# One tile of a gather stage handled in two halves of 64 tokens, with its small pieces of work moved between the dots

## The reference

```
q      = (xt @ wq).reshape(T, 8, 2, 128)
scores = einsum('thcd,hcnd->thcn', q, keys)
s_top, i_top = top_k(scores, 16)
cand     = s_top[:, :, 0, :, None] + s_top[:, :, 1, None, :]
best, pos = top_k(cand.reshape(T, 8, 256), 16)       # idx = the 16 experts of each head
gate = softmax(best)
hid  = gelu(einsum('td,thkd->thk', xb, U[idx]))      # U: 16384 x 2048
out  = einsum('thk,thkd->td', gate * hid, Vt[idx])   # Vt: 16384 x 2048
```

## Time and profile before

| | us |
|---|---|
| median of 3 runs | 2131.49 |
| lowest and highest | 2127.75, 2134.61 |
| profiled execution, its own time | 2132.88 |
| its span | 2131.1 |
| PE busy | 1480.5 (69%) |
| DVE busy | 1619.7 (76%) |
| ACT busy | 872.1 (41%) |
| POOL busy | 969.6 (46%) |

### The profile page before, as it was taken

One profiled execution on the slowest core, in us unless ns is written; L12 is line 12 of the kernel. 1 busy time (PEld: TensorE's weight loads), 2 busy tenths in 40 slices (PEclk: granted clock), 3 DMA queues, 4 the chain that ended last, 5 costly groups with the idle time before them and its releaser, 6 DMA issues.

```text
span 2131.1 us, 26457 instructions
## 1 busy us (share of the span) xinstructions
PE 1480.5 (69%) x9809; PEld 1371.6 (64%) x9809; DVE 1619.7 (76%) x2122; ACT 872.1 (41%) x1116; POOL 969.6 (46%) x699
## 2 busy tenths in 40 slices
PE   6999999999999999910000002211358999999997
PEld 6987998898999889910000002211347999999996
DVE  5465764545644556789999999877888999899997
ACT  4354432344333444211211226577655444444443
POOL 1002220000000000178888878888866776667763
PEclk9999999999999999965555555555589999999998
DMA  5555344434455554699999999999917999999996
GB/s 202 177 178 194 139 139 138 153 135 158 158 178 178 198 178 167 250 361 422 421 422 408 416 369 411 412 421 417 419 52 263 357 358 358 350 358 359 359 358 229
DMA packets 151818, 597.85 MB, mean 281 GB/s; under 512 B 14720, under 2 KB 14736, under 8 KB 118288
## 3 DMA queue, kind: packets, MB, share of 16 engines
q0 software_dynamic: 58048, 356.02, 42.0%
q1 hardware_dynamic: 93648, 240.22, 32.0%
HBM read 594.09 MB, written 2.10 MB: 280 GB/s over the span
## 4 chain that ended last, share of the span: by engine, by line
PE 47%; issue 20%; POOL 13%; DVE 13%; DMA 5%; ACT 1%; POOLq 0%; DVEq 0%; SPq 0%; ACTq 0%; PEldq 0%
PE acc L1608 8%; PE acc L1611 8%; PE acc L1610 8%; POOL slots L495 6%; POOL starts L534 5%; DVE slots L1397 5%; PE acc L1625 3%; PE acc L1627 3%; PE acc L1626 3%; DMA starts<-in_v_gather,expert 2%; DMA slots<-in_peer_u,expert 2%; PE acc L1922 2%; PE scr L1924 2%; PE acc L1924 2%; PE scr L1922 2%
## 5 line engine op out<-in xcount | busy, mean ns | idle before, releaser
L881 DVE TENSOR_TENSOR w_lo<-raw,w_hi 128x2048 fp32r<-128x2048 f32 x136 | 314.7, 2315 | 302.8 <-ACT w_hi L550 301.8
L1397 DVE SCALAR_TENSOR_TENSOR slots<-slots,acc 128x2048 f32<-128x2048 f32 x188 | 424.7, 2285 | 46.6 <-DMA slots<-in_peer_u,expert 44.4
L550 ACT ACTIVATE w_hi<-raw 128x2048 fp32r<-128x2048 f32 x136 | 260.1, 1913 | 428.7 <-PE acc L1611 286.5
L534 POOL DMA_INDIRECT starts<-in_v_gather,expert x256 | 343.8, 1343 | 158.9 <-issue 81.3
L495 POOL DMA_INDIRECT slots<-in_peer_u,expert x256 | 250.9, 980 | 260.6 <-DVE expert L1369 148.4
L1608 PE MATMUL acc<-hT_hi,w_hi 128*128 128x256 f32 x1024 | 294.6, 288 | 3.0 <-PE acc L1611 1.7
L503 POOL TENSOR_TENSOR slots<-slots,N 128x2048 f32<-128x2048 f32 x62 | 280.7, 4528 | 31.5 <-DMA slots<-in_peer_u,expert 31.2
L843 ACT ACTIVATE v_hi<-v_raw 128x1408 fp32r<-128x1408 f32 x128 | 177.0, 1384 | 284.3 <-PE scr L1924 213.1
L1610 PE MATMUL acc<-hT_lo,w_hi 128*128 128x256 f32 x1024 | 292.1, 285 | 0.0
L1611 PE MATMUL acc<-hT_hi,w_lo 128*128 128x256 f32 x1024 | 291.9, 285 | 0.0
L746 ACT ACTIVATE slots<-slots 128x2048 f32<-128x2048 f32 x62 | 118.4, 1910 | 366.7 <-POOL slots L503 366.7
(11 more groups left out here) (284 smaller groups left out, 3341.9 us busy)
## 6 DMA issues: line engine op xcount, KB each, us to landing
raw<-in_w_in SPq DMA_DIRECT2D x88, 1024.0 KB
v_raw<-in_v_dense SPq DMA_DIRECT2D x128, 704.0 KB
raw<-in_w_o SPq DMA_DIRECT2D x16, 1024.0 KB
raw<-in_peer_wq SPq DMA_DIRECT2D x16, 1024.0 KB
raw<-in_w_a_up SPq DMA_DIRECT2D x8, 1024.0 KB
raw<-in_w_b_up SPq DMA_DIRECT2D x8, 1024.0 KB
slots<-in_peer_u,expert POOLq DMA_INDIRECT x256, 9.2
starts<-in_v_gather,expert POOLq DMA_INDIRECT x256
```

What stands on the lines that cost most here:

```text
L534: pool.indirect_dma_start(starts[s % CRING][:, :], None, v_gather[:, :], bass.IndirectOffsetOnAxis(ap=expert[:, s // NSEL, s % NSEL:s % NS ...
L550: a.activation(w_hi[:, m % 2, :, :], raw[:, m % 2, :, :], ACT.Copy).then_inc(hi_ready, 1)
L881: v.tensor_tensor(w_lo[:, m % 2, :, :], raw[:, m % 2, :, :], w_hi[:, m % 2, :, :].bitcast(fp32), ALU.subtract).then_inc(lo_ready, 1)
L1397: v.scalar_tensor_tensor(out=slots[j][:, :], in0=slots[j][:, :], scalar=1.0, in1=row, op0=ALU.mult, op1=ALU.mult, accum_out=hid_sum[:, t, ...
```

## The change

Tile 1 is gathered in two halves. In the first half (q = 128 to 191, phase 1) the 128 partitions hold tokens 0 to 63 of the tile twice, and a gather brings two choices of each of 64 tokens; in the second (q = 192 to 255, phase 2) the same for tokens 64 to 127. The number of gathers and their size stay.

- SP makes the doubled indices (`expert_twice`) and copies: tokens 0 to 63 of N1 twice into a new buffer `rows_twice`, then tokens 64 to 127 of N1 over tokens 0 to 63. In phase 1 ACT also copies `rows_twice` to N1's tile 0, for POOL's products.
- `rows_to_psum` runs three times, for phases 0, 1 and 2.
- The dots of a half lie on two sets of partitions; PE brings them together (`fold_hid`), once for the first half and once for both, and DVE reads the result from PSUM.
- `weights` is cut into `shift_gate`, `scale_gate`, `curve_in` and `curve_out`, which stand in groups 29, 30, 32 and 33 for tile 0, in groups 46, 47, 48 and 49 for tile 1's softmax and its first half; the last curve stands after the last dot.
- 48 of the 64 batches of scatters stand in the gather stage: one a group from 35, two a group from 43 to 62. 16 stay behind the last dot. POOL makes the first one-hots of most of them as soon as rows 249 and 250 are used; two are made ahead by ACT in groups 62 and 63.
- The ring of row buffers is ten to q = 123, eight to q = 203, and from q = 204 seven in the order of LATE_ROWS, three of them new. Row 127 goes to DVE, not to POOL.
- `weight_of1` is laid out by halves, [2, 128, 64]; `e_hi` and `e_lo` read it so.

```diff
+FIRST_TEN, LAST_TEN = 10, 124
+LAST_EIGHT = 204
+LATE_ROWS = (6, 7, 8, 11, 12, 9, 10)
+PHASES = (0, NSEL, NSEL + NSEL // 2, GATHERS)
+IN_GATHERS = SCATTERS - BATCHES // 2
-SPREAD_FROM, SPREAD_TWICE = 35, 57
+SPREAD_FROM, SPREAD_TWICE, SPREAD_END = 35, 43, 63
-AHEAD_FROM = 47
+AHEAD_FROM, AHEAD = 62, 2
+SHIFTED_AT = (29, 46)
...
     if q < LAST_TEN:
-        return (q - FOUR) % len(ROW_AT)
-    return 2 + (q - LAST_TEN) % SLOTS
+        return (q - FOUR) % FIRST_TEN
+    if q < LAST_EIGHT:
+        return 2 + (q - LAST_TEN) % SLOTS
+    return LATE_ROWS[(q - LAST_EIGHT) % len(LATE_ROWS)]
...
+    def until(g):
+        late = SPREAD_END - SPREAD_TWICE
+        return (max(0, min(g, SPREAD_TWICE) - SPREAD_FROM)
+                + max(0, min(g, SPREAD_END) - SPREAD_TWICE) * (IN_GATHERS - SPREAD_TWICE + SPREAD_FROM) // late)
+
+    return range(until(g), until(g + 1))
+
+def weighted_first(n):
+    return n < IN_GATHERS and (n < ACT_WEIGHTS or n % 3 == 0)
...
+            def double_experts(pair):
+                sp.wait_ge(expert_ready, 4 + pair + 1)
...
+                for u in range(2):
+                    for r in range(2):
+                        sp.dma_start(expert_twice[r * HALF:(r + 1) * HALF, u, cs]...
+            double_experts(0)
+            sp.wait_ge(h2_ready, NT)
+            for r in range(2):
+                sp.dma_start(rows_twice[r * HALF:(r + 1) * HALF, :], N1[0:HALF, 1, :]).then_inc(rows_in, 16)
+            sp.wait_ge(rows_in, 32)
+            sp.dma_start(N1[0:HALF, 1, :], N1[HALF:P, 1, :]).then_inc(rows_in, 16)
...
+            for j in (11, 12):
+                pool.wait_ge(row_used[j], uses_before(GATHERS, j))
+            for n in range(AHEAD, BATCHES // 2):
                 if maker(n) == "pool":
...
+            def curve_in(w):
+                z, h = dots_of(w), hid[:, 0, :]
+                if w:
+                    dve.wait_ge(hid_landed, w)
+                    link(v.tensor_copy(z, hid_ps))
...
+                link(v.tensor_tensor(h, z, z, ALU.mult))
+                link(v.tensor_scalar(h, h, TANH_A * TANH_B, TANH_A, ALU.mult, ALU.add))
+                v.tensor_tensor(h, h, z, ALU.mult).then_inc(tanh_in, 1)
...
             for i in range(GROUPS):
                 for q in range(FOUR * i, FOUR * i + FOUR):
                     if q >= FOUR and not on_pool(q):
                         dot(q)
+                    if q % FOUR == 0 and q in (PHASES[1] + FOUR, PHASES[2] + FOUR):
+                        curve_out(phase_of(q) - 1)
...
-                if i == GROUPS // 2 + 1:
-                    weights(0)
-                    dve.sem_inc(h_used, 1)
-                if i == GROUPS // 2 + 2:
-                    copy_gate(0)
+                for t in range(NT):
+                    if i == SHIFTED_AT[t]:
+                        shift_gate(t)
+                    if i == SHIFTED_AT[t] + 1:
+                        scale_gate(t)
+                    if i == PHASES[t + 1] // FOUR + 1:
+                        copy_gate(t)
                 if i == IJ_GROUP:
                     copy_ij(1)
-                for n in spread(i):
-                    hot_second(0, n)
-            weights(1)
+                for m in spread(i):
+                    hot_second(m)
+                for w in range(NT):
+                    if i == PHASES[w + 1] // FOUR:
+                        curve_in(w)
+            curve_in(2)
+            curve_out(2)
...
+            def fold_hid(w):
+                pe.wait_ge(ij_ready, NT)
+                pe.wait_ge(gateT_ready, w)
...
+                for r in range(2):
+                    rows = slice(r * HALF, (r + 1) * HALF)
+                    to = hid_ps.rearrange("p (h r k) -> p h r k", h=H, r=2)[:, :, r, :]
+                    for u in range(w):
+                        last = t_.matmul(to, (ident if u == r else turned)[rows, :], ...
+                    if r == 0:
+                        last.then_inc(half_folded, 1)
+                        pe.wait_ge(half_folded, w)
+                last.then_inc(hid_landed, 1)
...
-            for n in range(BATCHES):
-                if n == spread(IJ_GROUP)[0]:
+            for m in range(IN_GATHERS):
+                if m == spread(IJ_GROUP)[0]:
                     turn_ij(1)
-                scatter(0, n)
-            turn_gate(1)
-            for n in range(BATCHES):
-                scatter(1, n)
+                if m == spread(PHASES[2] // FOUR + 1)[0]:
+                    fold_hid(1)
+                    turn_gate(1)
+                scatter(m)
+            fold_hid(2)
+            turn_gate(2)
+            for m in range(IN_GATHERS, SCATTERS):
+                scatter(m)
```

More of the change, by code:

```diff
@@ L260, in build @@
         hot_a, hot_b = carve("hot_a", 2, SC, P), carve("hot_b", 2, SC, P)
[L261 removed]
+        hot_a1 = [at(f"hot_a1_{n}", kib, [SC, P]) for n, kib in enumerate(PLACE_AT)]
         spot = [0]
@@ L485, in gather @@
                 t, k, j = q // NSEL, q % NSEL, buffer_of(q)
-                if k % (2 * TOPK) == 0:
+                index = expert_twice[:, k // HALF, k % HALF:k % HALF + 1] if t else expert[:, 0, k:k + 1]
+                if t == 0 and k % (2 * TOPK) == 0:
                     pool.wait_ge(expert_ready, q // (2 * TOPK) + 1)
+                if t and k < HALF and k % TOPK == 0:
+                    pool.wait_ge(experts_in[k // TOPK], 64)
+                if j == 10 and not uses_before(q, j):
+                    pool.wait_ge(product_ready, sum(map(on_pool, range(PHASES[2]))))
+                if j == 12 and not uses_before(q, j):
+                    pool.wait_ge(ij_ready, NT)
                 if q == 0:
@@ L728, in _, with rows_to_psum @@
                     hi(G_WQ + 2, m, i, 4)
-            def rows_to_psum(t):
+            def rows_to_psum(phase):
                 act.wait_ge(h2_ready, NT)
-                if t:
-                    for q in range(NSEL - SLOTS, NSEL):
+                if phase:
+                    act.wait_ge(rows_in, (32, 48)[phase - 1])
+                    for q in range(PHASES[phase] - SLOTS, PHASES[phase]):
                         if not on_pool(q):
@@ L736, in rows_to_psum @@
                 for half in range(2):
-                    if t == 0:
+                    if phase == 0:
                         act.wait_ge(acc_free[half], 1 + G_END // 2)
-                    a.activation(acc[:, half, :], N1[:, t, half * 2 * GW:(half + 1) * 2 * GW], ACT.Copy
+                    src = rows_twice if phase == 1 else N1[:, phase // 2, :]
+                    a.activation(acc[:, half, :], src[:, half * 2 * GW:(half + 1) * 2 * GW], ACT.Copy
                                  ).then_inc(h2_rows, 1)
+                if phase == 1:
+                    act.wait_ge(product_ready, sum(map(on_pool, range(NSEL))))
+                    a.activation(N1[:, 0, :], rows_twice[:, :], ACT.Copy).then_inc(rows_copied, 1)
             def sum_product(q):
@@ L826, in high_e @@
                 q, at0 = 2 * pair // (P // PIECES), 2 * pair % (P // PIECES)
-                for t in range(NT):
-                    last = a.activation(e_hi[:, pair % 2, t, :],
-                                        weight_of[t][q][:, at0:at0 + 2, :].rearrange("p a s -> p (a s)"), ACT.Copy)
+                a.activation(e_hi[:, pair % 2, 0, :],
+                             weight_of0[q][:, at0:at0 + 2, :].rearrange("p a s -> p (a s)"), ACT.Copy)
+                last = a.activation(e_hi[:, pair % 2, 1, :].rearrange("p (a u s) -> p u a s", a=2, u=2),
+                                    weight_of1[:, :, 2 * pair:2 * pair + 2, :], ACT.Copy)
                 last.then_inc(e_hi_ready, 1)
@@ new lines, in fold_hid @@
+            def fold_hid(w):
+                pe.wait_ge(ij_ready, NT)
+                pe.wait_ge(gateT_ready, w)
+                for j in range(len(ROW_AT)):
+                    if uses_before(PHASES[w + 1], j):
+                        pe.wait_ge(row_used[j], uses_before(PHASES[w + 1], j))
+                for r in range(2):
+                    rows = slice(r * HALF, (r + 1) * HALF)
+                    to = hid_ps.rearrange("p (h r k) -> p h r k", h=H, r=2)[:, :, r, :]
+                    for u in range(w):
+                        last = t_.matmul(to, (ident if u == r else turned)[rows, :],
+                                         hid_sum[rows, 1, u * HALF:(u + 1) * HALF].rearrange("p (h k) -> p h k", h=H),
+                                         start=u == 0, stop=u == w - 1)
+                    if r == 0:
+                        last.then_inc(half_folded, 1)
+                        pe.wait_ge(half_folded, w)
+                last.then_inc(hid_landed, 1)
@@ L1886, in scatter @@
+            def scatter(m):
+                pe.wait_ge(scattered, 1 + m)
+                n = m - IN_GATHERS
+                if m < IN_GATHERS:
+                    pe.wait_ge(a_ready[0], m + 1)
                 else:
                     by = maker(n)
-                    earlier = sum(maker(m) == by for m in range(PLACES, n + 1))
```

(5 more changed lines are left out.)

249 lines of the change are left out of this document (145 added, 104 removed).

## The result

The changed kernel is a little slower: the ratio of its time to the time before is 1.0043, with a 95% interval of 1.0029 to 1.0057. The medians are 2141.65 us (20 runs, 2136.36 to 2152.23) and 2132.39 us (20 runs, 2123.97 to 2141.68). The forecast was 2121.5, with a range of 2105 to 2137: the time lies outside it, on the slow side, by 4.7 us.

The account below looks back on a forecast made before the run. Bounds: often-full DMA engines in the gather stage, a tail of weights and scatters, PE in the dense stage. Terms -22.2 + 11 - 3 + 3 + 1 = -10.2 from 2132.9 give 2122.7, as median 2121.5 us; range 2105 to 2137.

Parts of the forecast that it names:

- The tail: Last dot to first dense matmul: 16 of 32 scatter batches leave, 36.6 us in place of 58.8, so -22.2.
- DMA added: Gather stage, about group 22: row copies of 1.5 MB and index packets cost +3, bounds 1 and 8.
- Index latency costs nothing: At gather(176): pair 3's indices, written in group 41, are first used some 15 us on, so no cost.
- Row 192: Phase change: DVE waits for the fold and gather(204) for row 200's dot; +11, bounds 0 and 15.
- Row 128: Phase change: weights cut into pieces hold DVE 8.6 us in place of 12.0; -3, bounds -9.3 and +3.
- Two batches a group: Groups 43 to 62: DVE's 9.1 and ACT's 8.8 us fit in 9.93; cost 0, upper bound +12.
- the seven rows: From row 204 on seven buffers: gather(4n+6) needs the sum of product 4n-1; +1, bounds 0 and 5.
- rival B: From group 43 on ACT becomes the bound, 11.3 us a turn adds 27; +17, 2148 us; chance 0.10.
- Rival A: The stop at row 192 is short, +2 in the sum; -20, 2111 us; chance 0.20.
- rival C: Nearly nothing left: row 192 costs 15, the seven rows 3, row 128 gains nothing; 0, 2131 us; chance 0.20.
- the two signs that I gave for being wrong: The gather stage is not longer, or the tail keeps more than 40 us.

Follow-up runs that it names:

- e1_turned: Changed kernel, with VectorE's two copies into turned made before it waits for the normalised rows; median 2139.28 us, 1.0022 of the kernel before.
- e6_before_full: Kernel before, plus 1.5 MB of unread copies as one of 128 partitions and one of 128 partitions and half the columns; 2134.42 us, ratio 1.0015.
- e5_before_half: Kernel before, plus the changed kernel's three row copies of 64 partitions into a buffer nothing reads; 2141.86 us, ratio 1.0047.
- e2_copies: Changed kernel, with the three row copies issued as soon as the normalised rows are ready; median 2131.51 us, 0.9996 of the kernel before.
- e3_fold: Changed kernel, with TensorE's second fold before batch 18's scatter instead of batch 20's; median 2136.82 us, 1.0021 of the kernel before.
- e8_fold_ring: Changed kernel, with the second fold two batches earlier and the late ring started with 11, 12, 10; median 2132.52 us, 1.0007 of the kernel before.
- e7_all: Changed kernel, with the edits of e1_turned, e2_copies, e3_fold and e4_ring together; median 2113.14 us, 0.9915 of the kernel before.
- e10_curve: e7_all, with ScalarE's tanh of the second part ahead of the two batches of group 48; median 2109.09 us, 0.9900 of the kernel before.
- e4_ring: Changed kernel, with the late buffer ring started with 11, 12, 10 in place of 6, 7, 8; median 2133.46 us, 1.0009 of the kernel before.
- e11_parts: e10_curve, with VectorE's later selection parts four in three groups, not five in four; median 2103.85 us, 0.9869 of the kernel before.

## Why the prediction was wrong

The mechanisms were mostly right; three sizes were off on the same side, and one cost was not in the sum. By its steps, predicted and measured:

- **The tail, -22.2: right, -23.0.** 16 batches cost 23.8 us from the first scatter's start to the last one's end, against 24.1. Two small parts were wrong and nearly cancel (the first scatter comes 7.7 us after the last dot, predicted 8.3): the fold with DVE's copy takes 3.3 us, not 1.95, because PE starts it 0.7 us behind the dot and its two halves follow each other with the wait between; and POOL's one-hots hold DVE not at all. DVE's operations on two SBUF operands behind the fold take 0.29 to 0.39 us (1592.02 above is one) where alone the like takes 0.29, while POOL makes one-hots in a row. I had +1.5 for it. The rule of the Trainium skill, "SBUF — State Buffer", section "Who interferes with whom", held beside POOL's products (4.47 us in the earlier trace rows, and z*z with 1.87 us at 1433.13). The one-hots read SBUF too, and by the rule they should hold DVE; no wait of that kind shows beside these short operations of one tensor operand, so the measurement decides, and I carried the rule too far. The copy of 3.38 us under e1_turned has one input and is no case of this rule of two; why the product holds it is not shown.
- **DMA added, +3: the step that failed most, +12.1.** I priced 1.5 MB at the gathers' rate. That price is right for copies of 128 partitions: e6_before_full measures 3.6 us where I had worked out 3.7. The changed kernel's copies have 64 partitions at each end, and e5_before_half measures 9.8 for the same bytes; the upper bound of 8, "copies at half rate", was already too low. In the prediction stood the rule of the Trainium skill, the same page, section "Door 1: The DMA port swizzle", that 64 adjacent partitions reach half of the ports, with an estimate of 4.8. The two experiments agree with its direction. Its estimate counted only what is written; measured is twice that. What I had at nothing is the effect on the gathers beside the copies: their packets of 8 KB take 0.59 us in place of 0.33 while such copies run (under e5_before_half). Why they do, and whether reading and writing on the same half add up, is open; if reads simply added up, the full copies should have cost more than their written bytes too. The other 2.3 us of the 12.1 come with the row copies as well, since moving them alone takes back 11.6 (e2_copies) and leaves the index copies in place. In the changed kernel the second copy lands 22.1 us after its issue, in e5_before_half both by 14.5; no run shows why.
- **The two copies into turned, not in the sum: +3.4** (e1_turned). I listed no price for the set-up of a constant, though the earlier trace rows shows what a POOL product does to a DVE operation beside it. Alone they cost 0.4 us.
- **"Index latency costs nothing": wrong, about 3 us** in the changed kernel (3.26 us at gather 176). I took 15 us of slack. It is 9.7: SP issues the last index copies from 1351.05 on, POOL wants them at 1360.80, and they are there at 1364.06, some 13 us after the first issue. A wait of 2.7 to 4.0 us shows in six profiles (e1_turned, e3_fold, e8_fold_ring, e7_all, e10_curve and the changed kernel), none in e2_copies and e4_ring, though e4_ring is the same program up to gather 204: it is there in one execution and not in another. In e11_parts the copies are issued 31 us ahead of the gather, and it does not wait.
- **Row 192, +11 with an upper bound of 15: right in mechanism, but 16.0 in size, above the bound.** By pieces of the gathers: 192 to 200 takes 22.6 us against 19.9, 200 to 204 takes 22.5 against 10.6, 204 to 208 takes 11.3 against 9.9. The tie that I worked out, gather 204 behind row 200's dot, is 11.9 (worked out: 10.8). What I left out is around it: 2.7 in front, where POOL's issue of a gather lasts 3.16 us in place of 0.95 while DVE runs its dots on the copy in SBUF, and 1.4 behind it. e3_fold, e4_ring and e10_curve show three ties in a row: the fold behind two batches on PE, the tanh behind two batches on ACT, the buffer. I had the tanh nowhere; in the changed kernel the first wait hid it.
- **Row 128, -3: -4.7**, in the right direction and within its bounds. No experiment splits it.
- **Two batches a group, 0, and the seven rows, +1: right.** POOL's products start at 1486.22, 1496.15 and 1506.08, 9.93 us apart as in the earlier trace rows, and 208 to the last dot is +1.3. So rival B (ACT as the bound) did not happen. Rival A did not either.

The outcome is nearest to rival C, nearly nothing left, which had 0.20, but it came by other terms: C let row 192 cost 15 and the seven rows 3, gave row 128 no gain, and left the copies at 3 (its last +1 has no term named). The copies, the indices and `turned` together are 15 us above their terms; row 128, which gained 4.7 after all, and the seven rows take some of that back. Neither of the two signs that I gave for being wrong came (a gather stage that is not longer, a tail over 40 us): both look at terms that were right in direction. The chance of 0.12 for slower was too small for a change that adds work of unmeasured price in three places to a stage where, as the stretches show, a late gather is not made up later.

## What to carry to other kernels

In a stage where transfers and engines wait for each other without slack, nothing that is added is free (the copies into `turned` cost 3.4 us where the DMA share of the kernel before was only 0.79, from 900 to 940): price each copy, each set-up operation and each new wait at its worst row, or put it where the engines have room, as e2_copies does for 10 us at no cost. When an engine waits in a chain of three engines, look for the next wait behind the first, because removing one only uncovers it; the order of the work on the waited-for engine (two batches ahead of the fold, two ahead of the tanh) is what to change. A plan that moves work out of a tail is worth its price only if the stage that receives it keeps its rate; here the same plan gives 0.43% loss or 1.3% gain depending on six such places.

## What the runs showed of the hardware

- Copies from SBUF to SBUF beside full gathers: 1.5 MB cost 9.8 us with 64 partitions at each end and 3.6 with 128. The DMA share is 1.01 in both; the bytes a second (334 and 422 GB/s from 1140 to 1160) show the difference. A gather's packet of 8 KB takes 0.59 us beside the former and 0.32 beside the latter.
- A POOL product on two SBUF operands holds a DVE copy of 64 columns for 3.38 us (alone 0.19). POOL's one-hots (one tensor operand, 0.58 us each) leave DVE's operations on two SBUF operands at 0.29 to 0.39 us.
- POOL's issue of a gather takes 0.95 us, and 3.16 us beside a DVE dot with two SBUF operands (1415.47).
- Stretches of unchanged work differ by several us between executions (the issue of gather 8 comes at 908 to 916 us, the dense stage takes 511.5 to 519.0), so an effect of 3 us has to be read from its own stretch, not from the span.
